# A two-layer decoder trunk on one Trainium2 core: one product of 512 columns for the high and the low activations in the retrieval's query projection and in the direct half of its first table

## The reference, cut to what matters

```python
q = (xb @ w_q).reshape(T, PEER_HEADS, 2, PEER_HALF)            # query projection
s = jnp.einsum('thpc,hpnc->thpn', q, keys)                     # key scores
sv, si = lax.top_k(s, PEER_TOPK)
cand = (sv[:, :, 0, :, None] + sv[:, :, 1, None, :]).reshape(T, PEER_HEADS, PEER_TOPK * PEER_TOPK)
cv, ci = lax.top_k(cand, PEER_TOPK)
...
g = jax.nn.softmax(cv, axis=-1)
u = jnp.take(u_tab, eid, axis=0)
a = jnp.einsum('td,thkd->thk', xb, u)                          # first table
coef = g * jax.nn.gelu(a, approximate=False)
vv = jnp.take(v_tab, eid, axis=0)
return jnp.einsum('thk,thkd->td', coef, vv)                    # second table
```

## Time and profile before

| | |
|---|---|
| median of three runs | 3901.87 us (3900.09 to 3905.02) |
| the profiled execution: time, span | 3898.5 us, 3895.7 us |
| TensorE busy | 3871.5 us, 99% |
| VectorE busy | 2516.7 us, 65% |
| ScalarE busy | 2094.0 us, 54% |
| TensorE's products | 25484 |
| granted TensorE clock, mean | 0.998 |

### The profile page before, as it was taken

The page is one execution under the profiler, slowest core; times in us unless marked ns, Lnnn a source line. Parts: engine busy times, 40 slices in busy tenths (PEclk is TensorE's granted clock), DMA queues, the critical chain, the costliest instruction groups (busy, mean ns, idle before and its releaser), DMA issues.

```text
span 3895.7 us, 72477 instructions
## 1 busy us (share of the span) xinstructions
PE 3871.5 (99%) x25484; PEld 3556.0 (91%) x25484; DVE 2516.7 (65%) x3845; ACT 2094.0 (54%) x3368; POOL 170.8 (4%) x148
## 2 busy tenths in 40 slices
PE   9999999999999999999999999999999999999999
PEld 8989999999998888888899889999999998888887
DVE  4565688778886555555565555778788875555555
ACT  5354444478885444444454544444688874444444
POOL 2110000010000000000121000000100000000000
PEclk9999999999999999999999999999999999999999
DMA  5445555555545566655454455555555455666665
GB/s 201 146 168 179 181 181 182 183 173 169 171 169 185 195 197 198 197 194 195 164 176 145 168 176 188 182 183 183 178 168 172 168 176 193 197 200 201 200 196 182
DMA packets 194870, 706.80 MB, mean 181 GB/s; under 512 B 22256, under 2 KB 22448, under 8 KB 194400
## 3 DMA queue, kind: packets, MB, share of 16 engines
q1 hardware_dynamic: 190800, 692.21, 53.7%
q0 software_dynamic: 3984, 13.37, 0.9%
HBM read 699.20 MB, written 6.29 MB: 181 GB/s over the span
## 4 chain that ended last, share of the span: by engine, by line
PE 98%; DVE 1%; DMA 1%; ACT 1%; issue 0%; DVEq 0%; SPq 0%; ACTq 0%
PE ps L1658 17%; PE ps L1659 17%; PE ps L1660 17%; PE ps L2042 12%; PE ps L2044 12%; PE ps L2043 12%; PE ps L2026 2%; PE ps L1741 1%; PE ps L1743 1%; PE ps L1742 1%; PE ps L1950 1%; PE ps L1949 1%; PE ps L1951 1%; PE ps L1726 1%; PE ps L1880 0%; DVE act_lo_t L1125 0%
## 5 line engine op out<-in xcount | busy, mean ns | idle before, releaser
L1066 DVE TENSOR_TENSOR w_lo<-w_raw,w_hi 128x1024 fp32r<-128x1024 f32 x1312 | 1628.1, 1243 | 1261.1 <-ACT w_hi L565 1245.9
L565 ACT ACTIVATE w_hi<-w_raw 128x1024 fp32r<-128x1024 f32 x1312 | 1389.6, 1060 | 1333.0 <-DMA w_raw<-in_v_tab 759.6
L1658 PE MATMUL ps<-act_lo_t,w_hi 128*128 128x256 f32 x5504 | 1562.9, 284 | 4.3 <-DVE act_lo_t L1125 3.1
L1659 PE MATMUL ps<-act_hi_t,w_lo 128*128 128x256 f32 x5504 | 1557.9, 283 | 0.0
L1660 PE MATMUL ps<-act_hi_t,w_hi 128*128 128x256 f32 x5504 | 1556.5, 283 | 0.0
L1658 PEld LDWEIGHTS ps<-act_lo_t,w_hi 128*128 128x128 f32 x5504 | 1053.8, 191 | 8.2 <-issue 6.3
L1660 PEld LDWEIGHTS ps<-act_hi_t,w_hi 128*128 128x128 f32 x5504 | 1055.4, 192 | 0.0
L1659 PEld LDWEIGHTS ps<-act_hi_t,w_lo 128*128 128x128 f32 x5504 | 1054.9, 192 | 0.1
L2042 PE MATMUL ps<-w_hi,act_lo_t 128*128 128x512 f32 x2048 | 797.8, 390 | 0.1
L2043 PE MATMUL ps<-w_lo,act_hi_t 128*128 128x512 f32 x2048 | 796.9, 389 | 0.0
L2044 PE MATMUL ps<-w_hi,act_hi_t 128*128 128x512 f32 x2048 | 796.9, 389 | 0.0
(11 more groups left out here) (242 smaller groups left out, 2211.7 us busy)
## 6 DMA issues: line engine op xcount, KB each, us to landing
w_raw<-in_u SPq DMA_DIRECT2D x512, 512.0 KB, 3.2
w_raw<-in_v_tab SPq DMA_DIRECT2D x512, 512.0 KB, 3.7
w_raw<-in_dense SPq DMA_DIRECT2D x288, 512.0 KB, 3.3
x_spill<-big POOLq DMA_DIRECT2D x16, 256.0 KB, 4.4
big<-x_spill POOLq DMA_DIRECT2D x32, 128.0 KB, 4.0
big<-in_x_in SPq DMA_DIRECT2D x4, 512.0 KB, 4.7
big<-in_keys POOLq DMA_DIRECT2D x2, 1024.0 KB, 7.6
out<-big SPq DMA_DIRECT2D x8, 256.0 KB, 2.1
```

The source lines that it names most:

```text
L565: act.activation(w_hi[:, slot, :], w_raw[:, slot, :], ACT.Copy).then_inc(s_hi, 1)
L1066: dve.tensor_tensor(w_lo[:, slot, :], w_raw[:, slot, :], w_hi[:, slot, :].bitcast(F32), ALU.subtract).then_inc(s_lo, 1)
L1658: pe.matmul(out, wh, xl, start=start, stop=False, **kw)
L1659: pe.matmul(out, wl, xh, start=False, stop=False, **kw)
```

## The change

The high and low activations now lie interleaved in one tile `act_t` [128, 16, 2, 256]. In the query projection and in the direct half of the first table (`wide=True`), each k is done by two products: `two_wide` streams high and low activations, 512 columns, through the high weights into a whole bank, and the high activations, 256 columns, through the low weights into its first half. So the bank's second half holds a part that has to be added. For each such block ScalarE copies the second half to SBUF (`aside`), VectorE adds it to the first half (`join`), and then, in the direct half, ScalarE takes the gelu from the bank (`gelu`). In the query projection the join itself writes the result and frees the bank. Two new semaphores carry this, `s_aside` and `s_joined`. The joins are put behind every second `lo`. Further, a load of ScalarE's table (`root_table`) moves behind the first eight blocks of the second table, and one copy of 256 columns beside the softmax goes.

```diff
@@ -62,6 +62,8 @@
...
 WPARTS = 2
+COUNT0 = {("wq", 0): 0, ("u", 0): 16, ("wq", 1): 16 + DIRECT, ("u", 1): 32 + DIRECT}
@@ -132,8 +134,8 @@
...
         big = sb("big", [P, 32768])
-        act_hi_t = sb("act_hi_t", [P, KB, T], F32R)
-        act_lo_t = sb("act_lo_t", [P, KB, T], F32R)
+        act_t = sb("act_t", [P, KB, 2, T], F32R)
+        act_hi_t, act_lo_t = act_t[:, :, 0, :], act_t[:, :, 1, :]
         ring_base = nc.sbuf_base
@@ -183,6 +185,8 @@
...
         s_used = S("s_used")
+        s_aside = S("s_aside")
+        s_joined = S("s_joined")
         s_evac = S("s_evac")
@@ -907,7 +911,7 @@
...
                         act.wait_ge(s_sc_ps, b + 16 * layer)
-                    act.activation(at(K_QS + T * par, T), bank(par, T), ACT.Copy).then_inc(s_evac, 1)
+                    act.activation(at(K_QS + T * par, T), bank(par, T), ACT.Copy).then_inc(s_aside, 1)
@@ -932,24 +936,40 @@
...
-                def ge(b, par, first=False):
+                def direct(b):
+                    return at(b * T, T) if isinstance(b, int) else big[:, bass.ds(b * T, T)]
+                def aside(b, par):
                     act.wait_ge(s_used, b * 2 + (ubase + 2))
-                    dst = at(b * T, T) if isinstance(b, int) else big[:, bass.ds(b * T, T)]
-                    act.activation(dst, bank(par, T), ACT.Gelu).then_inc(s_evac, 1)
+                    act.activation(direct(b), ps[:, par, T:2 * T], ACT.Copy).then_inc(s_aside, 1)
+                def joined(b):
+                    act.wait_ge(s_joined, b + (DIRECT * layer + 1))
+                def gelu(b, par):
+                    act.activation(direct(b), bank(par, T), ACT.Gelu).then_inc(s_evac, 1)
                 act.wait_ge(s_spill, 16 * PIECES * (layer + 1))
-                ge(0, 0)
+                aside(0, 0)
                 for s in range(4):
+                    if s % 2 == 0:
+                        joined(s // 2)
                     hi(s, ubase + 4 + s)
                     if s % 2:
-                        ge(s // 2 + 1, (s // 2 + 1) % 2)
+                        aside(s // 2 + 1, 1 - s // 2)
+                    else:
+                        gelu(s // 2, s // 2)
...
                     for s in range(8):
+                        if s % 2 == 0:
+                            joined(i * 4 + (s // 2 - 2))
                         hi(s % 4, i * 8 + (ubase + s))
                         if s % 2:
-                            ge(i * 4 + (s // 2 - 1), (s // 2 + 1) % 2)
+                            aside(i * 4 + (s // 2 - 1), 1 - s // 2 % 2)
+                        else:
+                            gelu(i * 4 + (s // 2 - 2), s // 2 % 2)
                 with act.Fori(1, SC_FIRST - 1) as i:
@@ -986,10 +1006,16 @@
...
                         weighted(i, s)
+                        if isinstance(i, int) and i == SC_FIRST and s == 0:
+                            joined(DIRECT - 2)
+                            gelu(DIRECT - 2, 0)
+                        if isinstance(i, int) and i == SC_FIRST and s == 2:
+                            joined(DIRECT - 1)
+                            gelu(DIRECT - 1, 1)
                         if s % 2:
...
                             if isinstance(b, int) and b < DIRECT:
-                                ge(b, b % 2)
+                                aside(b, b % 2)
                             else:
@@ -1016,7 +1042,6 @@
...
                 c_hi(1, 1)
-                root_table()
                 hi(2, vbase + 2)
@@ -1026,6 +1051,7 @@
...
                 v_blocks(0, range(2, V_TURN))
+                root_table()
                 act.wait_ge(s_mix, (N_KEYS - DIRECT) * (layer + 1))
@@ -1066,15 +1092,35 @@
...
-            def ahead(n0):
+            def join(name, layer, b, par):
+                dve.wait_ge(s_aside, b + (COUNT0[name, layer] + 1))
+                if name == "wq":
+                    dst = at(K_QS + T * par, T)
+                else:
+                    dst = at(b * T, T) if isinstance(b, int) else big[:, bass.ds(b * T, T)]
+                if name == "u":
+                    dve.tensor_tensor(bank(par, T), bank(par, T), dst, ALU.add).then_inc(s_joined, 1)
+                else:
+                    dve.tensor_tensor(dst, dst, ps[:, par, T:2 * T], ALU.add).then_inc(s_evac, 1)
+            def ahead(n0, before=None):
                 for s in range(RING):
                     lo(s, n0 + s)
+                    if before and s == 1:
+                        join(*before, 1)
...
                 n0 = SLAB0[name, layer]
+                if name == "wq":
+                    join(name, layer, 0, 0)
                 with dve.Fori(1, nslabs // RING) as i:
...
                         lo(s, i * RING + (n0 + s))
+                        if s % 2 and name == "wq":
+                            join(name, layer, i * 2 + (s // 2 - 1), 1 - s // 2)
@@ -1442,7 +1488,8 @@
...
-                def topk_turn(item, n0, slabs):
+                def topk_turn(item, n0, slabs, name, first):
@@ -1453,26 +1500,30 @@
...
                                 steps.pop(0)()
+                        if s % 2:
+                            join(name, layer, first + s // 2, 1 - s // 2 % 2)
                 qbase = SLAB0["wq", layer]
-                with dve.Fori(1, 4) as i:
-                    for s in range(RING):
-                        lo(s, i * RING + (qbase + s))
+                stream("wq", layer, 16)
...
                     dve.wait_ge(s_sc, 16 * layer + 2 * item + 3)
-                    topk_turn(item, qbase + 16 + 8 * item, range(8))
-                ahead(ubase)
+                    topk_turn(item, qbase + 16 + 8 * item, range(8), "wq", 7 + 4 * item)
+                ahead(ubase, ("wq", layer, 15))
                 dve.wait_ge(s_sc, 16 * (layer + 1) + 1)
+                join("u", layer, 0, 0)
                 for s in range(RING):
                     lo(s, ubase + RING + s)
+                    if s % 2:
+                        join("u", layer, 1 + s // 2, 1 - s // 2)
                 with dve.Fori(1, ITEMS - 1) as i:
-                    topk_turn(i + 1, i * 8 + ubase, range(8))
+                    topk_turn(i + 1, i * 8 + ubase, range(8), "u", i * 4 - 1)
...
                 lo(1, ubase + 8 * (SC_FIRST - 1) + 1)
+                join("u", layer, DIRECT - 5, 1)
                 dve.wait_ge(s_cexp, layer + 1)
@@ -1480,12 +1531,13 @@
...
                     lo(s % 4, ubase + 8 * (SC_FIRST - 1) + s)
+                    if s % 2:
+                        join("u", layer, DIRECT - 5 + s // 2, 1 - s // 2 % 2)
...
                 dve.tensor_copy(jt[:, :, :].rearrange("p c t -> p (c t)"), bank(3))
-                chain(dve.tensor_copy(rstd[:, :], bank(4, T)))
-                chain(dve.tensor_copy(jw[:, 0, :], rstd[:, :]))
-                chain(dve.tensor_tensor(jw[:, 1, :], rstd[:, :], jw[:, 0, :].bitcast(F32), ALU.subtract))
+                chain(dve.tensor_copy(jw[:, 0, :], bank(4, T)))
+                chain(dve.tensor_tensor(jw[:, 1, :], bank(4, T), jw[:, 0, :].bitcast(F32), ALU.subtract))
@@ -1535,6 +1587,8 @@
...
                         lo(s % 4, i * 8 + (ubase + 8 * SC_FIRST + s))
+                        if isinstance(i, int) and i == 0 and s == 1:
+                            join("u", layer, DIRECT - 1, 1)
                         if s % 2 == 0 and pair:
@@ -1547,6 +1601,7 @@
...
                     lo(s % 4, ubase + 8 * (SC_FIRST - 1) + s)
+                join("u", layer, DIRECT - 2, 0)
                 scatter_turn(0)
@@ -1659,13 +1714,21 @@
...
-            def half_block(slot, n, b, half, fill=None):
+            def two_wide(b, wh, wl, kb):
+                pe.matmul(bank(b), wh, act_t[:, kb, :, :], start=kb == 0, stop=False)
+                return pe.matmul(bank(b, T), wl, act_hi_t[:, kb, :], start=False, stop=kb == KB - 1)
+            def half_block(slot, n, b, half, fill=None, wide=False):
                 pe.wait_ge(s_lo, n + 1)
...
                     c = slice(P * k, P * (k + 1))
+                    if wide:
+                        ins = two_wide(b, w_hi[:, slot, c], w_lo[:, slot, c], kb)
+                        continue
                     ins = three(ps[:, b, 0:T], w_hi[:, slot, c], w_lo[:, slot, c], act_hi_t[:, kb, :],
@@ -1683,7 +1746,8 @@
...
                         s = 2 * par + half
-                        half_block(s, i * 4 + (n0 + s), par, half, fill if first and par == 0 else None)
+                        half_block(s, i * 4 + (n0 + s), par, half, fill if first and par == 0 else None,
+                                   wide=name == "wq")
                 blk(0, 0, True)
@@ -1982,7 +2046,7 @@
...
                             s = 2 * b + half
-                            half_block(s % 4, i * 8 + (u0_ + s), b % 2, half)
+                            half_block(s % 4, i * 8 + (u0_ + s), b % 2, half, wide=True)
                             if after:
```

## The result

The changed kernel takes 4007.78 us (median of 4 runs, 4004.97 to 4009.1) against 3900.98 us (3899.57 to 3905.02) for the one before: ratio 1.0271, 95% interval 1.0253 to 1.0289. It is 2.7% slower. The forecast was 3988 us in a range of 3960 to 4020. The profiled execution took 4008.07 us, 109.6 us more than the profiled one of before; its span is 4006.3 us, 110.7 more.

A forecast was written before the change was run, and what follows sets the result against it. VectorE, waiting for hi behind each join, was to replace TensorE as the bound in the direct half. 46.4 - 3.5 + 0.45 - 0.65 + 0.5 = +43.2 us per layer, +86.4 in both, gave 3988 us, range 3960 to 4020.

The forecast's parts named there:

- own terms, 28 and 6 us above 3988: Upward range terms in the direct-half loop: F up to 1.85 us gives +28, 0.2 us per item on VectorE's stretches 6.
- TensorE's products: Query projection and direct half: a k takes 345.9 ns, 13.7 less; 35.1 us saved in all if TensorE stays the bound.
- the joins stay hidden: Rival: in the direct half the joins' cost is hidden and TensorE stays the bound, 3868 us; chance 0.07.
- The round: VectorE's rounds in a direct-half item: 6.94, 7.61, 7.71 and 4.17 us, in all 26.4 against 23.0 for TensorE before.
- F: Time added to each VectorE round in the direct half by join, handoffs and hi: 1.60 us, ends 1.50 and 1.85.
- 3984.9: Forecast time in us of the profiled execution: 3898.5 before plus 86.4 for both layers.
- TensorE's gaps: Direct-half loop: TensorE idles about 2.0 us twice per item, ended by lo.
- The rest of a layer: Outside the direct-half loop, per layer: projection -3.5 us, last key score +0.45, blocks 0 to 2 -0.65, softmax +0.5.
- The tail around the softmax: Blocks 60 to 63: block 60 ends 6.4 us behind block 59, block 61 some 6.0 later; +0.5 us per layer.
- cancelled: Rival: gain and loss cancel at F = 0.75, an item takes 23.0 us, about 3896 to 3902 us; chance 0.03.
- The clock falls as well: Rival: gaps in the direct half also lower TensorE's clock, at worst 39 us more, between 3990 and 4027; chance 0.04.
- a granted clock below 1.00: Sign listed as showing the forecast wrong: TensorE's granted clock below 1.00 in the direct-half loop.

The follow-up runs named there:

- hi first: Changed kernel, but in the direct half ScalarE rounds hi of slab 2b+4 before it waits for join b, not after: 3880.0 us.
- join ahead: Changed kernel, but VectorE's join stands directly behind the lo of every second slab, ahead of the top-k steps there: 3882.25 us.
- the kernel with six fillers: Changed kernel plus six constant float32 products of 128x128 ahead of the third and fourth block of each item in the direct-half loop: 4003.76 us.
- the kernel with half the waits: Changed kernel, but in two of an item's four rounds in the direct-half loop hi comes before the wait for the join: 3931.7 us.

## Why the prediction was right

The mechanism is shown by removing it in two different ways (hi first: 3880.0; join ahead: 3882.25) and by halving it (3931.7). The forecast lies 20 us below the measured time, inside of its range (whose own terms, 28 and 6 us above 3988, end at 4022 and not at 4020). Three things of its working were off.

*TensorE's products.* The pair was to take 345.9 ns, by adding the paces of a stream of 512 and a stream of 256 columns. In the hi-first kernel it takes 352.8 on average. The starts tell why: in its window it is 236 ns from a wide to a narrow product and 117 from the narrow to the wide one (means), against 227 and 120 in the pure streams. The saving of 13.7 ns per k was mis-sized; it is 7 here and 10.5 in the projection. So only half of the fixed part of a product goes, or a little more, and the best case was never -35 us: the rival "the joins stay hidden" is what the hi-first kernel does, and that comes to -18 us, not -34.

*The round.* F was to be 1.60 us. The joins lasted 0.432 (0.415 taken). In two of the four rounds, where the wait has a row of its own in ScalarE's queue, hi started 0.12 to 0.14 us behind the end of the join (0.035 taken). The gap ahead of the join is 0.24 to 0.26 in three rounds, instead of 0.12, and two rows of VectorE's queue stand in it. The four rounds came to 7.14, 7.68, 7.89 and 4.13, against 6.94, 7.61, 7.71 and 4.17. An item takes 26.84 us in layer 0 and 26.96 in layer 1, where 26.4 was said. From join 2 to join 58, which are 14 items, it is 376.4 and 377.7 us against 14 x 26.4 = 369.6: 15 of the 23 us by which the profiled time lies above 3984.9. The two projections are 1.6 us dearer than forecast, for the price of the pair. Some 7 us lie in the mixers and the second tables of that one execution, where nothing was forecast. At most 4 of them can be the layout's, as said above; that the others are chance is the likeliest reading and no more.

*TensorE's gaps.* Said: two per item of 2.0 us, so some 4 us idle. The item shown has 1.80 and 1.88, but in the windows TensorE idles only 21.7 and 24.5 of 230 us, 2.5 and 2.9 per item. The rest of the forecast's 4 us went into the products at the lower clock. Where the clock is kept up, it is idle time again or fillers: 0.55 + 1.4 us, twice per item. The forecast was right about the room, and had not seen what would fill part of it.

*The rest of a layer.* The projection saved 2.4 us over 14 blocks, 0.17 each (0.22 said). The last key score waited 0.46 us longer (0.45 said). The tail around the softmax came out as worked: from join 58 to join 61 it is 17.9 us in layer 0 and 16.5 in layer 1, against 4.2 + 6.4 + 6.0 + 0.48 = 17.1 by the forecast's numbers. The number fits in part by luck: in layer 0 a stretch at the lower clock begins with join 58, TensorE is without a gap there (busy 30 of 30 us behind it), and in the kernel with six fillers, which has neither the stretch nor fillers in these blocks, it is 16.1 us. So where TensorE is the bound the lower clock does cost time, here some 1.8 us once.

*The rivals.* "Hidden" and "cancelled" didn't come. "The clock falls as well" came as far as the clock goes, and cost nothing in the loop: what TensorE loses, its next gap gives back, as the rival's own text had said for most of it. I had listed a granted clock below 1.00 as a sign that the forecast's picture was wrong. It is no such sign, since it says nothing about who is waited for. The Trainium skill ("TensorE: Matmul & The Clock Gate", section "HAM oscillation — how this bites in real kernels") tells of a kernel whose TensorE waits at every tile and then starts the tile at the lower clock. The trace agrees that the clock falls where TensorE keeps idling, 0.95 in the window against 1.00. In that section the lower clock is given a price, 26.7 of that kernel's 211 us. Here it has none in the loop, since the rounds are the same with a granted clock of 1.00.

## What to carry to other kernels

If a change hands a result through two engines, ask what stands behind each of its waits in the queues. Here an add of 0.43 us was waited for, a hi of 1.06 us stood behind that wait, and the engine that had just done the add needed this hi next. Work that another engine needs soon belongs ahead of such a wait, if it doesn't need the result itself. VectorE, busy 80% of the time, had room for the joins, but not for idling at four fixed places in each item as well.

## What the runs showed of the hardware

- In an alternating stream of 512 and 256 columns, each with its own weights, the starts lie 233 and 117 ns apart in the changed kernel (medians over all pairs) and 236 and 117 in the window of the hi-first kernel (means). A pair there takes 352.8 ns, 7 more than the pure streams' 226.0 and 119.85 add up to.
- Ahead of the join two rows stand in VectorE's queue, one of 0.04 to 0.05 us for an address and one of 0.065 to 0.075 with the wait. The gap there is 0.24 to 0.26 us, against 0.12 with one row of 0.04 ahead of a lo before. In the short round, whose lo ends later than these rows, there is no gap.
- TensorE's granted clock fell to its lower level for stretches of 3.4 us with gaps no longer than 2.0 us, at most two per item, and it fell 22 times in the direct halves of both layers, which hold 28 items. In the kernel with half the waits, which has one gap per item, most of them of 1.1 to 1.9 us, it fell three times, all in layer 1. With 1.4 us of each gap filled by other products it stayed at the upper level in the whole direct half.
